# A hybrid encoder step on one core: three moves in the hand-written order of the engines' work

## What is computed

```python
h = modulate(x, norm1_gain, sh1, sc1)
z = h @ w_in                                  # all projections at once
o_a, gla_state = gla_recurrence(q, k, v, log_a, gla_h0)
y_a = (rmsnorm(o_a, gla_gain) * silu(gr)) @ w_gla_out
p = softmax(s1) - lam * softmax(s2)           # block-causal for the prompt, 512 cached keys for the sample
y_b = (rmsnorm(p @ v, diff_gain) * (1 - lambda_init)) @ w_diff_out
x = x + gt1 * ((sigmoid(g_a) * y_a + sigmoid(g_b) * y_b) @ w_out)
h2 = modulate(x, norm2_gain, sh2, sc2)
# retrieval: top 16 of 128 + 128 key scores, then top 16 of their 256 sums
act = gelu(einsum('td,thkd->thk', h2, peer_u[idx]))
x = x + gt2 * einsum('thk,thkd->td', g * act, peer_v[idx])
```

## The kernel before

| engine | step b |
| --- | --- |
| TensorE | half of the lane, `weigh(b-1)`, the rest of the lane |
| ScalarE | `dots(b)`, lane |
| VectorE | `dots(b)`, `weigh(b-1)`, lane |
| SyncE | lane, `weigh(b)` (stores of y), loads for a new unit |

## Time and profile before

### The profile page before, as it was taken

The page is one execution under the profiler, slowest core; times in us unless marked ns, Lnnn a source line. Parts: engine busy times, 40 slices in busy tenths (PEclk is TensorE's granted clock), DMA queues, the critical chain, the costliest instruction groups (busy, mean ns, idle before and its releaser), DMA issues.

```text
span 4877.4 us, 46321 instructions
## 1 busy us (share of the span) xinstructions
PE 3150.4 (65%) x14944; PEld 1920.4 (39%) x14944; DVE 2692.1 (55%) x7493; ACT 1294.4 (27%) x2807; POOL 1253.0 (26%) x1067
## 2 busy tenths in 40 slices
PE   6887937885787278855974398775559753333333
PEld 4675735552565046523753064442237430000000
DVE  2133146677534766866345755565442456675675
ACT  2343103455310034635010225534330100000000
POOL 0000002322223233223222322222121224444453
PEclk8887978887888579967987598887679875555555
DMA  7322439997999799958998787865567878999998
GB/s 263 131 72 97 171 103 382 382 358 257 364 350 412 274 391 383 381 215 305 360 369 330 305 324 282 294 227 216 202 236 283 331 275 346 412 407 389 397 409 339
DMA packets 284681, 1466.27 MB, mean 301 GB/s; under 512 B 46344, under 2 KB 103528, under 8 KB 118392
## 3 DMA queue, kind: packets, MB, share of 16 engines
q0 software_dynamic: 152064, 1107.36, 58.1%
q1 hardware_dynamic: 132376, 355.94, 20.5%
HBM read 1426.39 MB, written 35.68 MB: 300 GB/s over the span
## 4 chain that ended last, share of the span: by engine, by line
PE 21%; DMA 18%; DVE 7%; issue 4%; ACT 2%; SPq 1%; POOL 0%; DVEq 0%; ACTq 0%; POOLq 0%
DMA rt_ring<-in_peer_uv,rt_few_idx 14%; PE pair L567 5%; PE rt_acc L807 4%; PE pair L556 3%; DVE rt_ring L1580 3%; PE bank L567 2%; PE bank L556 2%; PE pair L722 2%; DMA dense<-scratch_mod 1%; DMA w<-out_v_prompt 1%; DVE rt_diag L1591 1%; DMA w<-in_weights 1%; DMA w<-out_v_sample 1%; PE bank L736 1%; DVE negmax L1427 0%
## 5 line engine op out<-in xcount | busy, mean ns | idle before, releaser
L1633 POOL DMA_INDIRECT rt_ring<-in_peer_uv,rt_few_idx x1056 | 1249.7, 1183 | 3596.1 <-PE rt_acc L807 2664.1
L1580 DVE SCALAR_TENSOR_TENSOR rt_ring<-rt_ring,rt_h 128x1024 f32<-128x1024 f32 x1056 | 1265.4, 1220 | 498.3 <-DMA rt_ring<-in_peer_uv,rt_few_idx 477.8
L807 PE MATMUL rt_acc<-rt_ring,rt_diag 128*32 128x512 f32 x4224 | 810.2, 844 | 985.6 <-DVE rt_diag L1591 985.2
L1142 ACT ACTIVATE rt_act_dot<-rt_dot 128x2 f32<-128x2 f32 x528 | 106.9, 203 | 2333.5 <-DVE rt_ring L1580 2332.6
L807 PEld LDWEIGHTS rt_acc<-rt_ring,rt_diag 128*32 128x32 f32 x4224 | 101.5, 125 | 1430.7 <-DVE rt_diag L1591 1287.4
L567 PE MATMUL pair<-dense,w 128*128 128x256 f32 (+1 forms) x2336 | 557.4, 397 | 19.7 <-DMA w<-in_weights 16.9
L556 PE MATMUL pair<-w,dense 128*128 128x256 f32 (+1 forms) x2288 | 544.3, 396 | 16.2 <-DMA w<-in_weights 11.6
L567 PEld LDWEIGHTS pair<-dense,w 128*128 128x128 f32 x2336 | 449.8, 195 | 145.1 <-issue 47.5
L556 PEld LDWEIGHTS pair<-w,dense 128*128 128x128 f32 (+1 forms) x2288 | 427.3, 190 | 157.7 <-issue 63.7
L722 PE MATMUL pair<-w,dense 64*128 64x512 f32 (+3 forms) x448 | 152.7, 813 | 244.2 <-ACT dense L1081 111.5
L567 PE MATMUL bank<-dense,w 128*128 128x256 f32 (+1 forms) x1248 | 295.0, 393 | 1.5 <-ACT dense L1123 1.0
(11 more groups left out here) (236 smaller groups left out, 3149.2 us busy)
## 6 DMA issues: line engine op xcount, KB each, us to landing
w<-in_weights SPq DMA_DIRECT2D x232, 1024.0 KB, 7.7
rt_ring<-in_peer_uv,rt_few_idx POOLq DMA_INDIRECT x1056, 10.9
rt_h<-scratch_h SPq DMA_DIRECT2D x132, 128.0 KB
dense<-scratch_mod SPq DMA_DIRECT2D x18, 512.0 KB, 12.7
dense<-in_x_prompt SPq DMA_DIRECT2D x16, 512.0 KB, 9.1
scratch_scores<-dense SPq DMA_DIRECT2D x64, 128.0 KB, 6.1
rt_sc<-scratch_scores SPq DMA_DIRECT2D x8, 1024.0 KB, 8.7
rt_x<-scratch_x SPq DMA_DIRECT2D x132, 32.0 KB
```

What stands on the lines that cost most here:

```text
L807: mm = nc.tensor.matmul(acc[u % 2][a * T:(a + 1) * T, :], diag[b % 2][:, i, :], slot[:, D + c * BANK:D + (c + 1) * BANK], start=(q == 0), ...
L1142: nc.scalar.activation(act_dot[:, b % 2, :], dot[:, b % 2, :], ACT.Gelu).then_inc(gelued, 1)
L1580: dt = nc.vector.scalar_tensor_tensor(up, up, 1.0, h2[u % 2][:], ALU.mult, ALU.mult, accum_out=dot[:, b % 2, i:i + 1])
L1633: nc.gpsimd.indirect_dma_start(ring[n % RING][:], None, d["peer_uv"], bass.IndirectOffsetOnAxis(ap=few_idx[u % 2][:, c:c + 1], axis=0)).th ...
```

## The change

`order` gives ScalarE the lane first and `dots(b)` behind it. VectorE gets `dots(b)`, lane, `weigh(b)`; so it makes the diagonals of batch b at the end of step b and not behind the dots of batch b+1. TensorE's and SyncE's lists stay as they were (SyncE has no work for `dots`). In PE's `attend` the `apply` block moves, unchanged, from the end of the tick to its beginning, ahead of `out`, `turn` and `score`.

```diff
 def order(engine):
 
     fill, steps = sequence()
-    items, last = list(fill), NU * NB - 1
+    items = list(fill)
     for b, ticked, units in steps:
-        lane, half, cut, spent = [i for i, _ in ticked], sum(c for _, c in ticked) / 2, 0, 0.0
-        while cut < len(ticked) and spent < half:
-            spent += ticked[cut][1]
-            cut += 1
-        before = [("weigh", b - 1)] if b else []
+        lane = [i for i, _ in ticked]
         if engine == "tensor":
-            items += lane[:cut] + before + lane[cut:]
+            half, cut, spent = sum(c for _, c in ticked) / 2, 0, 0.0
+            while cut < len(ticked) and spent < half:
+                spent += ticked[cut][1]
+                cut += 1
+            items += lane[:cut] + ([("weigh", b - 1)] if b else []) + lane[cut:]
         elif engine == "scalar":
-            items += [("dots", b)] + lane
-        elif engine == "vector":
-            items += [("dots", b)] + before + lane
+            items += lane + [("dots", b)]
         else:
-            items += lane + [("weigh", b)] + units
-    return items + ([("weigh", last)] if engine in ("tensor", "vector") else [])
+            items += [("dots", b)] + lane + [("weigh", b)] + units
+    return items + ([("weigh", NU * NB - 1)] if engine == "tensor" else [])
...
                     for b in range(6):
                         pe.wait_ge(bank_free[b], counts[b])
+                if row["apply"] is not None:
+                    x, first, last, G = row["apply"]
...
+                    pe.wait_ge(at_copied, session_of[G] + 1)
+                    if first == 0:
+                        pe.wait_ge(at_rescaled, base + x)
+                    for kt, w in tiles[first:first + 4]:
+                        mm = nc.tensor.matmul(bank[5][0:n, 0:VD], mixT[0:w, G % 2, (kt - first) * P:(kt - first) * P + n], v[0:w, kt, :],
+                                              start=(kt == 0), stop=(kt == len(tiles) - 1))
+                    mm.then_inc(at_applied, 1)
+                    released[g, "kv" if t < NT else "kvs", h] = (at_applied, G + 1)
                 for h, s in row["out"]:
                     pe.wait_ge(at_gained, g * DH + h + 1)
...
-                if row["apply"] is not None:
-                    x, first, last, G = row["apply"]
...
-                    mm.then_inc(at_applied, 1)
-                    released[g, "kv" if t < NT else "kvs", h] = (at_applied, G + 1)
```

More of the change, by code:

```diff
@@ L688, in attend @@
                         pe.wait_ge(bank_free[b], counts[b])
+                if row["apply"] is not None:
+                    x, first, last, G = row["apply"]
+                    h, ti = units[x]
+                    t = GROUPS[g][ti]
+                    n, tiles = width(t), key_tiles(t)
+                    v = W[WPOS[g, "kv" if t < NT else "kvs", h] % NW][:, D:].rearrange("p (t c) -> p t c", c=VD)
+                    pe.wait_ge(at_copied, session_of[G] + 1)
[6 more added lines that the diff above has]
+                    released[g, "kv" if t < NT else "kvs", h] = (at_applied, G + 1)
                 for h, s in row["out"]:
@@ L725, in attend @@
                                 mm.then_inc(at_scored[m], 1)
-                if row["apply"] is not None:
-                    x, first, last, G = row["apply"]
-                    h, ti = units[x]
-                    t = GROUPS[g][ti]
-                    n, tiles = width(t), key_tiles(t)
-                    v = W[WPOS[g, "kv" if t < NT else "kvs", h] % NW][:, D:].rearrange("p (t c) -> p t c", c=VD)
-                    pe.wait_ge(at_copied, session_of[G] + 1)
-                    if first == 0:
-                        pe.wait_ge(at_rescaled, base + x)
-                    for kt, w in tiles[first:first + 4]:
-                        mm = nc.tensor.matmul(bank[5][0:n, 0:VD], mixT[0:w, G % 2, (kt - first) * P:(kt - first) * P + n], v[0:w, kt, :],
-                                              start=(kt == 0), stop=(kt == len(tiles) - 1))
-                    mm.then_inc(at_applied, 1)
-                    released[g, "kv" if t < NT else "kvs", h] = (at_applied, G + 1)
             def merge(g, i):
```

## The result

The changed kernel takes 4955.59 us (median of 4 runs, 4949.23 to 4960.73) against 4879.07 us of the kernel before in the same session; the ratio is 1.0149, 95% interval 1.0127 to 1.0172. It is slower by 76.5 us in the medians, 1.5%, which is clear of the noise. Forecast were 4821 us and a range of 4735 to 4920: the sign is wrong and the time lies outside the range.

The account below looks back on a forecast made before the run. Engine chains were taken to bound three attention stages, VectorE and ScalarE the scan, DMA the last stage, PE the merge. Terms -74 -40 -8 +4 +64 +10 -14 = -58 us gave 4821 us from 4879; range 4735 to 4920.

Parts of the forecast that it names:

- part c: PE's tick: value product ahead of transposes and scores frees the weight slot earlier, but waits for VectorE's rescale behind dots.
- first group: Attention ahead of all gathers: value product waits for the rescale, about 0.5 us a head, +4 us, bounds 0 and +10.
- done at 7.5: Third group's attention, first half of a head: exponentials end at 7.5 us, score 2.9 follows, 10.4 in all.
- 122 forecast: Gain of the second, third and last groups' attention together: 122 us.
- Second group's attention, -8 predicted: Load of 10 us bounds it; release to release 21.2 to 19.9 us, some six heads: -8, bounds -20 and +10.
- Third group's attention, -40 predicted: Two units a head; head shortens from 28.3 to 23.3 us, 5.0 saved a head: -40 us, bounds -60 and -10.
- Last group's attention, -74 predicted: Eight heads of three units; gaps between scores shrink, 9.3 us saved a head: -74 us, bounds -95 and -25.
- Scan stretches, +64 predicted: Six linear-attention stretches: VectorE waits for ScalarE's lane and Gelu, net 11 us each: +64, bounds +20 and +110.
- Norm, -14 predicted: Norm ticks of three groups: ScalarE makes rstd beside dots, saving 4 to 5 us each: -14, bounds -20 and 0.
- Rotary, +10 predicted: Rotary stages of keys and queries: weigh waits 1 to 2 us in some steps: +10 us, bounds 0 and +30.
- Lockstep decides: Rival: VectorE cannot run a batch ahead of ScalarE; scan, rotary and projection steps lose; 4940 us, chance 0.24.
- lower bounds: Smallest forecast attention gains: -25 us in the last group, -10 in the third, +10 (a loss) in the second.

Follow-up runs that it names:

- The lists: Kernel before with both new orders (ScalarE lane before dots, VectorE weigh at its step's end), value product still at the tick's end: 4880.78 us, ratio 1.0016.
- the ScalarE list alone: Kernel before with only ScalarE's new order (lane, then dots), VectorE's order and the value product's place as before: 4832.81 us, ratio 0.9930.
- the best parts: Kernel before with ScalarE's new order outside the scan steps and the value product between transposes and scores: 4764.75 us, ratio 0.9760.

## Why the prediction was wrong

- **The value product ahead of the tick (part c): the step that failed.** The prediction had it wait for "VectorE's rescale of the unit before, which is queued behind dots", priced it at 0.5 us a head in the first group, and otherwise took it as the move that frees the weight slot earlier. In the third and last group's sums the transposes do stand behind it, but not what follows: the exponentials are "done at 7.5", 0.5 us behind the transposes, in the one and missing in the other, and the second group's sum has neither transposes nor exponentials. The trace has the score 2.0 us behind the transposes' end (2291.05, then 2293.10), and the Gelu, the diagonals and the next dots stand behind the same exponentials. Shown by moving the value product behind the transposes alone: 112 us. With that place the three attention stages give 61 us, half of the 122 forecast. In the first group, where no gathers run, the prediction said +4; over the profiled executions with three buffers, the first batch starts at 757 us in the mean with the value product at the head (six kernels, 754 to 761) and at 746 us with it further back (nine kernels, 742 to 754, of which the kernel before is the latest). So it cost about 11 us there.
- **Second group's attention, -8 predicted, +33.7 measured.** "The load of 10 us bounds it" failed. A head holds 2.4 batches, not one, and the ring of rescale, transposes, exponentials, Gelu, diagonals and dots takes 9.2 us in the batch shown and 12.3 in the next: two rounds make the head of 21.5 us, and the load's waits, 39.5 us before, are gone. The lists' part is +9.9, the value product's +23.8.
- **Third group's attention, -40 predicted, +3.1 measured.** The lists give -30.6, near the forecast, and the value product takes 33.7 back. The cycle of three batches, where the stage holds 3.6 a head, is another part of the step; what it is worth was not measured.
- **Last group's attention, -74 predicted, -9.3 measured.** The step that failed is "the 6.3 us load lands at 9.7 [...] The load is hidden". The release came as worked out, the landing after 14 us. With half the gathers' bytes 17 us come back; the value product's place costs 30 (365.5 against 396.0), with the load as late. The prediction also had the wait for the short key set gone and that for the long one still there; it is the other way round (37.1 and 5.7 us). Three weight buffers gave 347.5 us at best, not the 335 predicted; the 292.4 us with four also lack load waits that the prediction left in.
- **Scan stretches, +64 predicted, +62.5 measured.** Right, by its own reasons. After, one step:

```profile
940.07 1.28 ACT L1140 ACT_TABLE_LOAD   x1
...
941.37 0.20 ACT L1140 ACTIVATE rt_act_dot<-rt_dot 128x2 f32<-128x2 f32 x1
941.60 0.51 DVE L1589 TENSOR_SCALAR rt_diag<-cst,rt_act_dot,rt_few_prob 128x32 f32<-128x32 f32 x2 [2.78 <-ACT rt_act_dot L1140]
```

  VectorE stands 2.78 us until the table load and the Gelu are done, then dots follow, where in the earlier trace rows they lay beside ScalarE's work. The Gelu starts 0.02 us behind the end of the load. The Trainium skill (ScalarE: Activation LUTs, "What ACT_TABLE_LOAD costs") adds 1.38 us of drain to each switch, about 40 us more in these stretches as an estimate; the trace shows none here, and the sum came out without it.
- **Norm, -14 predicted, +5.0 measured**, within the scatter of no change. VectorE still waits for rstd, 3.12 us where it was 3.30: 

```profile
1790.25 0.75 DVE L1223 TENSOR_SCALAR dense<-dense,nrstd 128x1024 f32<-128x1024 f32 x1 [3.12 <-ACT nrstd L892]
```

  **Rotary, +10 predicted, -3.6 measured**: keys +19.2, queries -22.8. I saw the loss in both and the gain in neither; the ScalarE list alone has the same two numbers (+17.3 and -22.8). What makes the queries gain was not tried.
- **The chances.** "Lockstep decides" had the right sign and 4940 us, with chance 0.24, but by another place: it had the loss outside attention and the attention at two thirds. Outside attention the changed kernel loses 53.5 us, less than that rival's 150, and attention lost 27.5 where the rival let it give 80: that its total is only 16 us from the measured one is luck. No rival had the value product as a cause. The range's upper end took the attention's gain for certain in part, although its lower bounds (-25, -10 and +10, together -25) with the scan's +110 would have led past it.

## What to carry to other kernels

A wait in an in-order queue costs what stands behind it, on this engine and then on the engines that wait for that: ask of a moved block first what it will hold up, and place it behind everything that is ready sooner. When batches of one loop are spread over the units of another, divide their numbers before pricing a cycle; a cycle read off one timeline can hold one batch where the mean is 2.4. And a small load's time to land is that of the moment at which it is issued: release it at another moment and its neighbours change.

## What the runs showed of the hardware that was not expected

The sample tile's load took 6.3 us to land with the last gathers issued 3.4 us ahead of it, and 14.2 (14.2 to 15.4 in five heads) with gathers issued 0.8 us ahead and 0.4 behind; in the best parts, with gathers 2.4 and 1.1 us ahead and none behind for 3.3 us, it took 8.2 to 9.1; with half the gathers' bytes PE waited for it once in the stage, 7.7 us, and not six times, 37.1. A ring of 8 rows instead of 9 made no difference that can be measured (4958.95 against 4955.59 us), though GpSimd waits over 2700 us for free rows.
